# The levels of two gated recurrences: 128-column stationary tiles, heads by turns in two row groups and two banks, and a projection in three parts

## What is computed

```python
def step(S, blk):
    qc, kc, vc, gc = blk
    b = jnp.cumsum(gc, axis=1)
    o_inter = jnp.einsum('bthk,bhkv->bthv', qc * jnp.exp(b), S)
    diff = b[:, :, None] - b[:, None, :]
    decay = jnp.exp(jnp.where(causal, diff, -jnp.inf))
    A = jnp.einsum('bthk,bshk,btshk->bths', qc, kc, decay)
    o_intra = jnp.einsum('bths,bshv->bthv', A, vc)
```

## Time and profile before

| | us |
|---|---|
| median of 3 runs | 1867.7 |
| lowest, highest | 1866.79, 1868.54 |
| the profiled execution: its time | 1867.47 |
| the profiled execution: its span, first to last instruction | 1865.7 |
| levels 0 to 6 of the first layer (186.9 to 278.1) | 91.2 |
| levels 0 to 6 of the second layer (1107.6 to 1206.4) | 98.8 |

### The profile page before, as it was taken

How to read it: one execution, slowest core, us unless ns; L and a number is a source line. 1 busy time by engine, 2 the same in 40 slices (tenths; PEclk the granted TensorE clock), 3 DMA queues, 4 the chain that set the end, 5 groups by cost and what they waited for, 6 DMA issues and landing times.

```text
span 1865.7 us, 35758 instructions
## 1 busy us (share of the span) xinstructions
PE 1769.5 (95%) x16070; PEld 1646.6 (88%) x16070; DVE 858.2 (46%) x1311; ACT 653.0 (35%) x963; POOL 71.1 (4%) x90
## 2 busy tenths in 40 slices
PE   6999998899999999999889999987999999999998
PEld 5988985588999999998888888845989999999988
DVE  5514885336423333346544157844354133333365
ACT  5422425544423222233344232245344231222233
POOL 0012110000000000000000130100000000000000
PEclk9999998899999999999989998988999999999999
DMA  7521428851836625442353132388419366355311
GB/s 265 179 68 60 160 82 338 306 179 69 310 125 216 217 101 205 158 137 68 111 206 110 58 132 77 123 336 297 155 64 317 123 214 217 110 193 181 123 58 63
DMA packets 60649, 303.67 MB, mean 163 GB/s; under 512 B 7120, under 2 KB 8784, under 8 KB 58832
## 3 DMA queue, kind: packets, MB, share of 16 engines
q1 hardware_dynamic: 53072, 200.91, 30.1%
q0 software_dynamic: 7424, 100.47, 15.4%
HBM read 290.74 MB, written 111.08 MB: 215 GB/s over the span
## 4 chain that ended last, share of the span: by engine, by line
PE 88%; DVE 7%; ACT 3%; issue 2%; DMA 1%; SPq 0%; DVEq 0%; ACTq 0%
PE pair L1684 15%; PE pair L1686 14%; PE pair L1685 14%; PE pair L887 3%; PE pair L738 3%; PE pair L740 2%; PE pair L742 2%; PE pair L720 2%; PE pair L670 2%; PE pair L721 2%; PE pair L722 2%; PE pair L671 2%; PE pair L672 2%; PE pair L1764 2%; PE pair L996 1%
## 5 line engine op out<-in xcount | busy, mean ns | idle before, releaser
L1684 PE MATMUL pair<-x_hi_part,w_hi_part 128*128 128x288 f32 x1088 | 322.2, 296 | 2.0 <-DVE tmp L2063 2.0
L1685 PE MATMUL pair<-x_lo_part,w_hi_part 128*128 128x288 f32 x1088 | 321.0, 295 | 0.0
L1686 PE MATMUL pair<-x_hi_part,w_lo_part 128*128 128x288 f32 x1088 | 319.9, 294 | 0.0
L2000 DVE TENSOR_TENSOR w_lo_part<-raw,w_hi_part 128x1024 fp32r<-128x1024 f32 x154 | 188.7, 1225 | 234.8 <-ACT w_hi_part L1851 234.8
L1684 PE MATMUL pair<-u_hi_part,w_hi_part 128*128 128x288 f32 x928 | 274.7, 296 | 0.0
L1685 PE MATMUL pair<-u_lo_part,w_hi_part 128*128 128x288 f32 x928 | 273.8, 295 | 0.0
L1686 PE MATMUL pair<-u_hi_part,w_lo_part 128*128 128x288 f32 x928 | 272.8, 294 | 0.0
L1851 ACT ACTIVATE w_hi_part<-raw 128x1024 fp32r<-128x1024 f32 x154 | 161.8, 1051 | 209.6 <-PE pair L1686 208.3
L1684 PEld LDWEIGHTS pair<-x_hi_part,w_hi_part 128*128 128x128 f32 x1088 | 203.9, 187 | 2.5 <-DVE tmp L2063 2.5
L1686 PEld LDWEIGHTS pair<-x_hi_part,w_lo_part 128*128 128x128 f32 x1088 | 204.9, 188 | 0.0
L1685 PEld LDWEIGHTS pair<-x_lo_part,w_hi_part 128*128 128x128 f32 x1088 | 204.3, 188 | 0.0
(11 more groups left out here) (282 smaller groups left out, 3552.3 us busy)
## 6 DMA issues: line engine op xcount, KB each, us to landing
raw<-w_units SPq DMA_DIRECT2D x210, 512.0 KB, 3.6
ck_out<-ck POOLq DMA_DIRECT2D x16, 3060.0 KB, 14.0
arena<-cv SPq DMA_DIRECT2D x24, 640.0 KB, 7.8
tail<-cv SPq DMA_DIRECT2D x24, 640.0 KB, 7.9
arena<-ck SPq DMA_DIRECT2D x18, 640.0 KB, 10.1
more<-ck SPq DMA_DIRECT2D x18, 640.0 KB, 12.9
h<-ck SPq DMA_DIRECT2D x12, 640.0 KB, 12.7
y_out<-h SPq DMA_DIRECT2D x16, 288.0 KB, 2.1
```

Source lines behind the costliest of these rows:

```text
L1684: nc.tensor.matmul(out, wh[:, cols], xh[:, k, t], start=n == 0, stop=False)
L1685: nc.tensor.matmul(out, wh[:, cols], xl[:, k, t], start=False, stop=False)
L1686: mm = nc.tensor.matmul(out, wl[:, cols], xh[:, k, t], start=False, stop=n == KT - 1)
L2000: return tt_(dst, src, hi.bitcast(F32), ALU.subtract).then_inc(*up(done, 1))
```

## The change

From level 1 on, the stationary tile holds the keys of two chunks (128 columns), and only the late queries of both chunks (64 columns, taken with a stride) are moved past it. One matmul so covers two chunks; of its output of 128 by 64 half is picked: the rows of a chunk against the queries of the same chunk. Level 0 keeps the 64 by 64 matmuls. The groups are taken as couples (0 and 1, 2 and 3, 4 and 5), whose heads stand in different rows and whose outputs stand in different banks, and the matmuls of the two groups stand by turns. A couple waits until both banks of the couple before are empty. The projection tile is cut at 18 and 33: 18 matmuls ahead of couple 1, 15 ahead of couple 2, 15 behind it. A pick from level 1 on is two instructions, each of 64 partitions and half the columns.

```diff
-                    for g, heads in enumerate(GROUPS):
-                        if l >= 4 and g in (2, 4):
-                            partners(2 * (l - 4) + g // 4)
-                        if g == 2 and l < len(LEVELS) - 1:
-                            project(5 + l, 0, 18)
-                        b_ = bank[4 + gi % 2]
+                    for first in range(0, len(GROUPS), 2):
+                        if l >= 4 and first >= 2:
+                            partners(2 * (l - 4) + first // 4)
+                        if first >= 2 and l < len(LEVELS) - 1:
+                            project(5 + l, *((0, 18) if first == 2 else (18, 33)))
                         if gi >= 2:
-                            pe.wait_ge(*at(lv_ev, gi - 1))
-                        for i, h in enumerate(heads):
-                            r, row, n = HEAD_AT[h]
-                            for c in range(NC):
-                                o = 64 * (c % 2)
-                                col = (4 * i + c // 2) * CH
-                                mm = nc.tensor.matmul(b_[o:o + 64, col:col + CH],
-                                                      kq[0][row:row + n, r, c * CH:(c + 1) * CH],
-                                                      kq[1][row:row + n, r, c * CH:(c + 1) * CH], start=True, stop=True)
-                        mm.then_inc(*up(lv_mm, 1))
-                        gi += 1
+                            pe.wait_ge(*at(lv_ev, gi))
+                        couple, n_heads = GROUPS[first:first + 2], len(GROUPS[first])
+
+                        for i in range(n_heads):
+                            for c2 in range(TT):
+                                for g, heads in enumerate(couple):
+                                    r, row, n = HEAD_AT[heads[i]]
+                                    b_, t, col = bank[4 + g], slice(2 * c2 * CH, 2 * (c2 + 1) * CH), (4 * i + c2) * CH
+                                    if l == 0:
+                                        for o in (0, 64):
+                                            one = slice(2 * c2 * CH + o, (2 * c2 + 1) * CH + o)
+                                            mm = nc.tensor.matmul(b_[o:o + 64, col:col + CH], kq[0][row:row + n, r, one],
+                                                                  kq[1][row:row + n, r, one], start=True, stop=True)
+                                    else:
+
+                                        late = kq[1][row:row + n, r, t].rearrange("p (b a e) -> p b a e", a=2, e=LEVELS[l])[:, :, 1]
+                                        mm = nc.tensor.matmul(b_[:, col:col + CH].rearrange("p (b e) -> p b e", e=LEVELS[l]),
+                                                              kq[0][row:row + n, r, t], late, start=True, stop=True)
+                                    if i == n_heads - 1 and c2 == TT - 1:
+                                        mm.then_inc(*up(lv_mm, 1))
+                        gi += 2
...
                     if l < len(LEVELS) - 1:
-                        project(5 + l, 18)
+                        project(5 + l, 33)
...
-                        nc.vector.copy_predicated(
-                            AT[:, s:s + n].rearrange("p s c t -> p (s c) t"), mask.to_broadcast([P, 4 * n, CH]),
-                            bank[4 + gi % 2][:, 0:4 * n * CH].rearrange("p (a t) -> p a t", t=CH)).then_inc(*up(lv_ev, 1))
+                        if l == 0:
+                            nc.vector.copy_predicated(
+                                AT[:, s:s + n].rearrange("p s c t -> p (s c) t"), mask.to_broadcast([P, 4 * n, CH]),
+                                bank[4 + gi % 2][:, 0:4 * n * CH].rearrange("p (a t) -> p a t", t=CH)).then_inc(*up(lv_ev, 1))
+                        else:
+
+                            e = LEVELS[l]
+                            late = mask.rearrange("p z (b a e) -> p z b a e", a=2, e=e)[:, :, :, 1]
+                            for par_ in range(2):
+                                rows = slice(64 * par_, 64 * par_ + 64)
+                                dst = AT[rows, s:s + n].rearrange("p s c (b a e) -> p (s c) b a e", a=2, e=e)[:, :, :, 1]
+                                src = bank[4 + gi % 2][rows, 0:4 * n * CH].rearrange("p (x z b e) -> p x z b e", z=2, e=e, b=CH // 2 // e)
+                                ins = nc.vector.copy_predicated(dst, late[rows].to_broadcast([64, 4 * n, CH // 2 // e, e]), src[:, :, par_])
+                            ins.then_inc(*up(lv_ev, 1))
```

More of the change, by code:

```diff
@@ L873, in _ @@
                         kq = (LV[l % 2], LV[l % 2])
-                    for g, heads in enumerate(GROUPS):
-                        if l >= 4 and g in (2, 4):
-                            partners(2 * (l - 4) + g // 4)
-                        if g == 2 and l < len(LEVELS) - 1:
-                            project(5 + l, 0, 18)
-                        b_ = bank[4 + gi % 2]
-                        if gi >= 2:
-                            pe.wait_ge(*at(lv_ev, gi - 1))
-                        for i, h in enumerate(heads):
-                            r, row, n = HEAD_AT[h]
-                            for c in range(NC):
-                                o = 64 * (c % 2)
-                                col = (4 * i + c // 2) * CH
-                                mm = nc.tensor.matmul(b_[o:o + 64, col:col + CH],
-                                                      kq[0][row:row + n, r, c * CH:(c + 1) * CH],
-                                                      kq[1][row:row + n, r, c * CH:(c + 1) * CH], start=True, stop=True)
-                        mm.then_inc(*up(lv_mm, 1))
-                        gi += 1
-                        if l in SMALL:
-                            b_ = bank[6 + si % 2]
-                            if si >= 2:
-                                pe.wait_ge(*at(ls_ev, si - 1))
-                            for i, h in enumerate(heads):
-                                r, row, n = HEAD_AT[h]
-                                mm = nc.tensor.matmul(b_[0:NEW, i * CH:(i + 1) * CH], kq[0][row:row + n, r, SEQ:T],
-                                                      kq[1][row:row + n, r, SEQ:T], start=True, stop=True)
-                            mm.then_inc(*up(ls_mm, 1))
-                            si += 1
@@ new lines, in _ @@
+                    for first in range(0, len(GROUPS), 2):
[3 more added lines that the diff above has]
+                            project(5 + l, *((0, 18) if first == 2 else (18, 33)))
+                        if gi >= 2:
+                            pe.wait_ge(*at(lv_ev, gi))
[17 more added lines that the diff above has]
+                        gi += 2
+                        if l in SMALL:
+                            for heads in couple:
+                                b_ = bank[6 + si % 2]
+                                if si >= 2:
+                                    pe.wait_ge(*at(ls_ev, si - 1))
+                                for i, h in enumerate(heads):
+                                    r, row, n = HEAD_AT[h]
+                                    mm = nc.tensor.matmul(b_[0:NEW, i * CH:(i + 1) * CH], kq[0][row:row + n, r, SEQ:T],
+                                                          kq[1][row:row + n, r, SEQ:T], start=True, stop=True)
+                                mm.then_inc(*up(ls_mm, 1))
+                                si += 1
```

## The result

The changed kernel takes 1911.62 us (median of 4 executions, 1909.47 to 1914.97) against 1868.12 us for the kernel before in the same comparison: ratio 1.0248, 95% interval 1.0225 to 1.027. It is 43.5 us slower, where 19 us were forecast; the time lies above the range of 1870 to 1903. The profiled execution has a span of 1911.4 us against 1865.7, 45.7 more.

What follows compares the result with a forecast made beforehand. TensorE was taken as the bound in the levels, VectorE having about 1 us to spare. 1867.7 + 16 (levels, with waits and picks) + 3 (clock) = 1887 us, range 1870 to 1903.

Steps and rivals of the forecast that it cites:

- Part 1, the matmuls: Levels 1 to 6: loading 128 weight columns sets the pace, a couple stays at 1.84 us, nothing gained beyond 0.05.
- The rivals that priced a couple at 0.94 or 2.6 us: 0.94: load not binding, 1871 us (0.12), or picks also cheaper, 1859 (0.05); 2.6: load and movement in turn, 1905 (0.07).
- Part 2, level 0: Level 0, four 64x64 tiles at once: couple 0.94 for 1.84 us by loads alone, but picks keep VectorE the bound.
- the walk: Step-by-step timing of TensorE and VectorE through each level at the rows' prices: 97.7 us a layer against 89.7, +8.0.
- Part 4, the waits: Levels: couples need both banks empty, VectorE idles before picks, TensorE waits 1.5 us at level starts; +16 us in all.
- the cover: Projection matmuls behind the last group, hiding VectorE's last picks and `scale`: 30 (3.95 us) before, 15 (2.17 us) after.
- the third rival: Matmuls of levels: load and movement of a 128-column tile in turn, couples 2.6 us, +18 a layer, 1905 us; chance 0.07.
- Part 3, the picks: VectorE picks as two instructions: 0.68 us a group for 0.64, 0.40 for 0.33 with one head, +0.3 us a level.
- Part 5, the clock: Stretches at 1.2 GHz within the levels, costing 10.6 us before: +3 us in all, between -6 and +15.

Runs made afterwards that it cites:

- the best version: Changed kernel with four 64x64 tiles throughout, projection 18/30, couple 1 in the projection tile's banks, single picks, late-half from level 3: 1839.39 us for 1866.29, ratio 0.9854.

## Why the prediction was wrong, by its own steps

**Part 1, the matmuls: right.** Couples of 1.94 us at full clock (1.79 to 1.84 forecast), weight loads of 187 ns, and with 64-column weights 0.98. The rivals that priced a couple at 0.94 or 2.6 us fall.

**Part 2, level 0: right, but for a small term.** Its couple takes 0.98 us (0.94 forecast), and the level ends with VectorE. The +0.5 us a layer that the walk put there did not come: 15.46 us for 15.42.

**Part 4, the waits: right in kind, nearly in size.** TensorE waits ahead of the levels for `scale`, VectorE ahead of the picks of couples 1 and 2. Of the 16 us forecast, 3.6 are the picks' +0.3 a level, 12.4 the waits and the cover. The run with the old picks has these alone: +12.6 in the levels with 7.3 us less of half clock, so 15 to 16 at full clock. Its level 4, for one, is 14.89 us, where 14.7 was forecast with the pick's 0.3 in it. A slip in the working went unpunished: VectorE's starts at level 1 add to 10.6 us of work and not to "all 11.9", which counts overlapping lengths; VectorE had more room there than the text says. (And the third rival adds up to 1904, not 1905.)

**Part 3, the picks: this step failed.** Forecast 0.68 us a group and 0.40 for a group of one head, +0.3 a level. Measured 1.51 and 0.93 at levels 1 and 2, 0.91 and 0.63 from level 3. By four and two of them: 6.04 + 1.86 = 7.9 us at levels 1 and 2 against 3.2 before (four at 0.64, two at 0.33), +4.7; and 4.9 against 3.2, +1.7, at each of the four others. The prices were taken from a 128x256 row and a 64x128 row, with whole rows as runs. None of the rows of before showed two instructions in a row that change between partitions 0 to 63 and 64 to 127, nor runs of one or two elements. The text named both ends for a couple's matmuls and none above 0.68 for a pick. A layer has 16.1 us more of picks, where 1.8 were forecast; part of it falls into waits that VectorE had anyway (level 4 grows by 0.6 at full clock, its picks by 1.7). Undoing the picks takes 32.8 of the 43.5 us away, the clock that falls with them included. Without the picks' term the forecast is 15.4, and 11.6 was measured: a little too high, not far too low.

**Part 5, the clock: this term was far too small.** +3 us forecast, with +15 as the far bound "if slow stretches double". They grew from 27.8 to 74.2 us, 2.7 times. At 0.3 to 0.47 us each the added 46.4 us cost an estimated 14 to 22. The forecast expected the waits to lower the clock and the third part of the projection to help, and both have support (half clock falls by 20 us when the waits are filled, and by 14 when only the third part is added). But the loss of clock comes with the longer picks: with the old ones the same order of matmuls has only 20.5 us at half clock. With picks at 0.68 the forecast could not see it. Why longer picks take the clock down so far is not shown; the waits of TensorE are a part of it, but in layer 1 filling them changed nothing.

The sum, as an estimate: 15 to 16 (waits and cover) + 14 to 22 (clock) + what is left for the longer picks at full clock, 8 to 17 = 46.4 measured in the levels. The forecast had 12.4, 3 and 3.6. Measured apart are only the two halves, 11.6 for everything but the picks and 32.8 for the picks with the clock that they bring down (44.4 together, since it is another comparison than the 43.5); the split of the second half rests on the factor above.

The Trainium skill, "TensorEngine Tiling (Array Packing)", section "PSUM Bottleneck", warns that once packing has made TensorE faster, copying out of PSUM may become the limit. The changed kernel is no case of it, since its couples are not faster (1.94 us). The run with four tiles of 64x64 points that way: couples at 0.98 us, and TensorE waits 1.46 us for VectorE ahead of level 2.

## What to carry to other kernels

Price a packed matmul by the columns of weights that it loads: 128 for 64 moving columns gives nothing, four tiles of 64x64 in different rows and banks give 1.9x. Before an operation is split to touch less data, look at the form of the pieces and at their neighbours: here half the data in two pieces cost 1.4 to 2.4 times as much, and one piece on all partitions with runs of at least four cost half. When two engines take turns over banks, look for a third pair that is free at that moment: with it and the longer cover the kernel went from 1863.51 to 1847.97 us. And when a time is split into shares, compare the same stretch at the same granted clock: level 2 before looked like 14.25 us and is 12.72.

## What the runs showed of the hardware

- VectorE's neighbouring instructions overlap by some 0.1 us (0.75 long, 0.64 to the next start), by 0.2 with short runs on 128 partitions (0.73 and 0.52). Where one works on partitions 0 to 63 and the next on 64 to 127, or the reverse, they don't: 0.72 to 0.74 long, the next 0.73 to 0.77 later. Two on partitions 0 to 63 do (0.29 long, 0.21 to the next start).
- `copy_predicated` of 256 columns lasts 0.73 us in runs of one or two elements and 0.43 in longer ones, on 64 partitions as on 128.
- Time at a granted 1.2 GHz within the levels: 28 us before, 74 after, 20.5 with the old picks, 7 in the best version, whose couples of small tiles take 1 us each. A us of it cost 0.33 to 0.47 us at levels 2 to 4 of the changed kernel (level 4: 18.71 for 15.50 us with 6.8 us of it), and nothing at level 0.
